# The first projection of a three-layer transformer step on one core: activations split straight out of PSUM, router product in fp32r, halved first weights, an early table load and eighteen warm-up products

## The reference, cut to what matters

```
xn = rms_norm(h, ln_mix[0])                  # 256 x 1024
splits = [q 1024, kc 256, vc 256, ks 256, vs 256, kw 256, vw 256, gl 48]
q, kc, vc, ks, vs, kw, vw, gl = split(xn @ w_in, splits)    # w_in: 1024 x 2608
gates = sigmoid(gl)                          # 48 gate columns
...
# then: compressed, selected and windowed attention, output projection, experts, ...
```

## Time and profile before

| | us |
|---|---|
| three timed runs | 1280.40, 1281.37, 1281.69 |
| median | 1281.37 |
| span of the profiled execution | 1282.1 |
| TensorE busy in it | 1207.8 (94%) |
| VectorE busy | 973.6 (76%) |
| ScalarE busy | 786.0 (61%) |
| first transpose starts | 6.69 |
| kv0 starts | 18.16 |
| q0 starts | 64.62 |

### The profile page before, as it was taken

The page is one execution under the profiler, slowest core; times in us unless marked ns, Lnnn a source line. Parts: engine busy times, 40 slices in busy tenths (PEclk is TensorE's granted clock), DMA queues, the critical chain, the costliest instruction groups (busy, mean ns, idle before and its releaser), DMA issues.

```text
span 1282.1 us, 15617 instructions
## 1 busy us (share of the span) xinstructions
PE 1207.8 (94%) x5843; PEld 982.8 (77%) x5843; DVE 973.6 (76%) x1347; ACT 786.0 (61%) x1166; POOL 25.2 (2%) x38
## 2 busy tenths in 40 slices
PE   6998998999999888989999998999998999999997
PEld 5887786888887677778788776887786887888886
DVE  4977848898987877779989886777777877675545
ACT  6467747677777677667777777443436566544343
POOL 0000000000000000000000000000001001000000
PEclk8998999999999999999999998999999999999999
DMA  8660213798996511339989935777785624467420
GB/s 318 242 264 1 66 67 140 289 370 343 357 372 236 230 71 67 137 142 386 363 346 368 349 116 209 287 284 287 290 327 230 258 120 146 167 278 286 164 99 34
DMA packets 41467, 291.84 MB, mean 228 GB/s; under 512 B 4736, under 2 KB 5120, under 8 KB 6576
## 3 DMA queue, kind: packets, MB, share of 16 engines
q1 hardware_dynamic: 40464, 287.82, 58.5%
q0 software_dynamic: 784, 2.63, 0.7%
q10 hardware_dynamic: 144, 0.39, 0.1%
HBM read 289.78 MB, written 1.05 MB: 227 GB/s over the span
## 4 chain that ended last, share of the span: by engine, by line
PE 62%; DVE 19%; ACT 10%; DMA 4%; issue 4%; POOL 0%; DVEq 0%; ACTq 0%; POOLq 0%
PE ps L430 17%; PE ps L432 17%; PE ps L431 17%; DVE wl L1659 6%; ACT wh L1173 4%; DMA ring<-stream_dram 4%; DVE AR L1889 3%; PE ps L625 1%; ACT AR L1295 1%; ACT XN L1196 1%; PE ps L985 1%; PE ps L458 1%; PE ps L578 1%; PE ps L626 1%; ACT XH L1228 1%
## 5 line engine op out<-in xcount | busy, mean ns | idle before, releaser
L1659 DVE TENSOR_TENSOR wl<-ring,wh 128x2048 fp32r<-128x2048 f32 x229 | 525.6, 2302 | 141.4 <-ACT wh L1173 138.0
L1173 ACT ACTIVATE wh<-ring 128x2048 fp32r<-128x2048 f32 x229 | 437.7, 1915 | 132.2 <-PE ps L432 67.2
L430 PE MATMUL ps<-wh,XH 128*128 128x512 f32 x1040 | 419.1, 403 | 13.0 <-DVE wl L1659 5.2
L432 PE MATMUL ps<-wh,XL 128*128 128x512 f32 x1040 | 408.0, 392 | 0.0
L431 PE MATMUL ps<-wl,XH 128*128 128x512 f32 x1040 | 407.1, 391 | 0.0
L430 PEld LDWEIGHTS ps<-wh,XH 128*128 128x128 f32 x1040 | 196.3, 189 | 61.6 <-issue 8.9
L432 PEld LDWEIGHTS ps<-wh,XL 128*128 128x128 f32 x1040 | 196.2, 189 | 43.0
L431 PEld LDWEIGHTS ps<-wl,XH 128*128 128x128 f32 x1040 | 196.7, 189 | 37.7 <-issue 0.7
L430 PE MATMUL ps<-wh,HT 128*128 128x512 f32 x360 | 142.0, 395 | 8.4 <-DVE XL L2085 4.5
L432 PE MATMUL ps<-wh,HT 128*128 128x512 f32 x360 | 140.4, 390 | 0.0
L431 PE MATMUL ps<-wl,HT 128*128 128x512 f32 x360 | 140.2, 389 | 0.0
(11 more groups left out here) (304 smaller groups left out, 1257.5 us busy)
## 6 DMA issues: line engine op xcount, KB each, us to landing
ring<-stream_dram SPq DMA_DIRECT2D x272, 1024.0 KB, 5.6
H<-x_dram SPq DMA_DIRECT2D x2, 512.0 KB, 4.9
out_dram<-XN SPq DMA_DIRECT2D x4, 256.0 KB, 2.0
XN<-ag_dram POOLq DMA_DIRECT2D x1, 768.0 KB, 5.1
AR<-pT_dram POOLq DMA_DIRECT2D x2, 256.0 KB, 2.9
AR<-g_final_dram POOLq DMA_DIRECT2D x1, 512.0 KB, 4.8
C<-cols_dram ACTq DMA_DIRECT2D x1, 385.0 KB, 4.6
ring<-stream_dram SPq DMA_DIRECT2D x2, 144.0 KB, 5.5
```

Source lines behind the costliest of these rows:

```text
L430: e.matmul(o, ah, bh, start=start, stop=False)
L432: return e.matmul(o, al, bh, start=False, stop=stop)
L1173: e.activation(wh[:, k % WBUF, :], ring[:, n % RING, :], ACT.Copy, scale=1.0).then_inc(up("whi", ("whi", k)))
L1659: e.tensor_tensor(wl[:, k % WBUF, :], ring[:, n % RING, :], h.bitcast(F32), ALU.subtract).then_inc(up("wlo", ("wlo", k)))
```

## The change

The transposes go on as before (`turn_rows`), but with no `XF` for this stage. ScalarE writes `XH = gain * bank` straight in fp32r (`high_all`), VectorE writes `XL = gain * bank - XH` straight from the bank (`low_all`, eight instructions in place of sixteen). The gates' weights are split too (`router_high`, `router_low`, 128x384), and their product is 24 fp32r products of 48 by 256 in place of the float32 one (`narrow_split`). Chunk 1 is split in two halves on ScalarE and VectorE, and kv0 begins behind the first half. The small activation that loads the square-root table stands at the head of ScalarE's program, before the wait for `cols`. TensorE issues 18 products of the identity with itself behind the wait for `cols` and ahead of the wait for x. Turning the gates back moves behind kv0. On ScalarE the copies of kv0 and the sigmoid and SiLU instructions now stand ahead of the third `take`, which splits chunk 5.

```diff
+WARM = 18
+        def router(n, part):
+            return TT_[:, 8 * n * part:8 * n * part + 8 * n]
 # tensor_program
-            def weights():
+            def weights(halved=False):
                 k = split_no[next_chunk()]
-                e.wait_ge(*at("wlo", k))
+                e.wait_ge(*(at("wlo half", k) if halved else at("wlo", k)))
...
+            def turn_rows(name, ready):
+                for label in ready:
+                    e.wait_ge(*at(*label))
+                for j in range(4):
+                    b = bank("fm", name, j, by=[("xs", name, 2 * j + 1)])
+                    for u in range(2):
+                        for t in range(TT):
+                            ins = e.transpose(b[:, 256 * u + 128 * t:256 * u + 128 * t + 128], H[:, t, 2 * j + u:D:8], ID)
+                    ins.then_inc(up("full", ("fm", name, j)))
+            def narrow_split(name, n):
+                next_chunk()
+                h, lo = (router(n, i).rearrange("p (t n) -> p t n", t=8) for i in range(2))
+                b = bank("narrow", name, by=[("nr", name)])
+                e.wait_ge(*at("rwl", name))
+                for k in range(8):
+                    e.wait_ge(*at("xs", name, k))
+                    ins = mm3(b[0:n, 0:256], (h[:, k, :], lo[:, k, :]), (XH[:, k, :], XL[:, k, :]), k == 0, k == 7)
+                ins.then_inc(up("full", ("narrow", name)))
...
 # project
+                            if halved and i + t == 0 and u == 2:
+                                e.wait_ge(*at("wlo", k))
 # tensor nsa()
-                feature_major_all("mix0", [("x", 0), ("x", 1)])
-                narrow("mix0", 48)
-                narrow_rows("mix0", 48, [("gt", 1)])
+                for i in range(WARM):
+                    e.matmul(PS[7][:, 0:128], IDR[:, :], IDR[:, :], start=True, stop=True)
+                turn_rows("mix0", [("x", 0), ("x", 1)])
+                narrow_split("mix0", 48)
...
-                project("kv0", "mix0", lambda t: [("kv", 0, t)])
+                project("kv0", "mix0", lambda t: [("kv", 0, t)], halved=True)
+                narrow_rows("mix0", 48, [("gt", 1)])
 # scalar_program
+            def high_all(name, gain, n, groups):
+                for i in groups:
+                    if i % 2 == 0:
+                        e.wait_ge(*at("fm", name, i // 2))
+                    e.activation(XH[:, i, :], ps("fm", name, i // 2)[:, 256 * (i % 2):256 * (i % 2) + 256], ACT.Copy,
+                                 scale=gain[:, i:i + 1]).then_inc(up("xraw", ("xh", name, i)))
+            def router_high(name, n, c):
+                e.wait_ge(*at("land", c))
+                e.activation(router(n, 0), ring[:, c % RING, 0:8 * n], ACT.Copy, scale=1.0).then_inc(up("act", ("rwh", name)))
+            def narrow_out(name, n):
+                e.wait_ge(*at("narrow", name))
+                e.activation(NR[0:n, :], ps("narrow", name)[0:n, 0:256], ACT.Copy, scale=1.0).then_inc(up("act", ("nr", name)))
 # scalar nsa()
-                feature_major_all("mix0", col("mix0", 0, 8))
-                narrow("mix0", 48)
+                high_all("mix0", col("mix0", 0, 8), 48, range(2))
+                router_high("mix0", 48, 0)
+                high_all("mix0", col("mix0", 0, 8), 48, range(2, 8))
+                n, more = chunks.due(AHEAD)
+                split_half(n, 0, 1)
+                split_half(n, 1, 1)
+                split([more])
+                narrow_out("mix0", 48)
                 split(chunks.one())
-                rms("mix0", lambda t, hf: ("x", t))
+                for t in range(TT):
+                    squares("mix0", t, lambda hf: ("x", t))
+                roots("mix0")
+                take()
+                e.wait_ge(*at("rs", "mix0"))
+                for t in range(TT):
+                    e.wait_ge(*at("pj", "kv0", t))
+                    e.activation(KV[:, t, half(0)], ps("pj", "kv0", t)[:, :], ACT.Copy, scale=rs(t)).then_inc(up("act", ("kv", 0, t)))
                 e.wait_ge(*at("rows", "mix0"))
-                e.wait_ge(*at("rs", "mix0"))
                 gv = ps("rows", "mix0")[:, 0:96].rearrange("p (a n) -> p a n", a=2)
...
-                kv_part(0)
+                take()
                 kv_part(1)
...
             e.wait_ge(*at("ident"))
+            warm("mix0")
             e.wait_ge(*at("cols"))
 # vector_program
+            def low_all(name, gain, groups):
+                for i in groups:
+                    e.wait_ge(*at("xh", name, i | 1))
+                    e.scalar_tensor_tensor(out=XL[:, i, :], in0=ps("fm", name, i // 2)[:, 256 * (i % 2):256 * (i % 2) + 256], scalar=gain[:, i:i + 1],
+                                           in1=XH[:, i, :].bitcast(F32), op0=ALU.mult, op1=ALU.subtract).then_inc(up("xsplit", ("xs", name, i)))
+            def router_low(name, n, c):
+                e.wait_ge(*at("rwh", name))
+                e.tensor_tensor(router(n, 1), ring[:, c % RING, 0:8 * n], router(n, 0).bitcast(F32), ALU.subtract).then_inc(up("dve", ("rwl", name), ("raw", c)))
 # vector nsa()
-                feature_major_all("mix0")
-                take()
+                low_all("mix0", col("mix0", 0, 8), range(2))
+                router_low("mix0", 48, 0)
+                low_all("mix0", col("mix0", 0, 8), range(2, 8))
+                n, more = chunks.due(AHEAD)
+                split_half(n, 0, 1)
+                split_half(n, 1, 1)
+                split([more])
                 split(chunks.one())
                 rms("mix0")
```

More of the change, by code:

```diff
@@ L496, in project_by_tile, with project @@
                             ins.then_inc(up("full", *labels))
-            def project(name, x, by, of=tuple(range(8)), between=None, part=(0, 1)):
+            def project(name, x, by, of=tuple(range(8)), between=None, part=(0, 1), halved=False):
                 if 0 in part:
@@ L503, in project @@
                 for i in part:
-                    k, h, l = weights()
+                    k, h, l = weights(halved and i == 0)
                     hv, lv = (v.rearrange("p (t n) -> p t n", t=4) for v in (h, l))
@@ L1481, in kv_part @@
                         e.activation(KV[:, t, half(c)], b[:, :], ACT.Copy, scale=rs(t)).then_inc(up("act", ("kv", c, t)))
-                        if c:
-                            e.activation(SQ[:, t, 256 * c - 256:256 * c], b[:, 0:256], ACT.Square, scale=rs(t)).then_inc(up("act", ("kvsq", c, t)))
+                        e.activation(SQ[:, t, 256 * c - 256:256 * c], b[:, 0:256], ACT.Square, scale=rs(t)).then_inc(up("act", ("kvsq", c, t)))
                 def first_layer(i):
```

## The result

| | before | changed |
|---|---|---|
| median, us | 1281.90 (10 runs) | 1285.07 (10 runs) |
| range | 1279.08 to 1284.20 | 1284.01 to 1286.32 |
| ratio | | 1.0020, 95% interval 1.0012 to 1.0028 |
| profiled execution: span | 1282.1 | 1283.7 (its own time 1285.76, so 2.06 lie around the span) |

The change is 3.2 us slower (1.5 to 3.6 by the interval) where 1.8 us faster was forecast. The forecast had given 0.08 to anything slower than 1283.9. In the profiled executions of all runs 2.0 to 2.2 us lie around the span, so the one of before, 1282.1, stood for 1284.1 to 1284.3, level with the two slowest of its ten (1284.08 and 1284.20). It was no typical execution.

A forecast was written before the change was run, and what follows sets the result against it. TensorE was taken to bound up to q0, VectorE 2.0 us behind. Start 1.9 + clock 3.1 - gates 0.25 - chunk 5 2.3 - VectorE at q0 0.45 = 1.95, rounded to 1.8: 1279.6 us, range 1277.9 to 1282.6.

The forecast's parts named there:

- the delay of the transposes: On TensorE ahead of kv0: 18 warm-ups end at 9.24, 2.55 us behind the arrival of x, and delay the transposes.
- the ready time of chunk 5: Second half of kv1: its split and low part are ready 8.0 us after the end of kv0.
- the wait of 2.3 us: In the middle of kv1: TensorE stands still 2.3 us for chunk 5, now split behind the copies of kv0.
- VectorE's bound at q0: At q0: VectorE has the first low part ready only at 62.65, TensorE would be there at 62.2; 0.45 us lost.
- Rival A: Ahead of kv0: warm-ups are cheap, 0.107 us each, kv0 starts at 15.45; gain 2.75 us, 1278.6; chance 0.25.
- Rival C: In kv0: the clock isn't held, kv0 begins at half clock, 3.1 us lost; 1282.5 us; chance 0.15.
- 3.1 (clock): In kv0: full clock in place of the half clock at its start gains 3.1 us.
- rival B: Behind the wait in kv1: the clock falls, TensorE loses 1.7 to 3.1 us; 1280.7 to 1282.1; chance 0.3.
- the likeliest case: Whole kernel: the summed terms hold, 1279.6 us (1278.9 to 1280.5); chance 0.3.
- the headline of my sum: At the end of kv0: 27.2 against 32.2, 5.0 us earlier, 1.9 by start and 3.1 by clock.

The follow-up runs named there:

- after_again: The changed kernel run once more with no edit, for a second profiled execution; median 1285.05 us, ratio to before 1.0020.
- before_late: The kernel before, with only ScalarE's copies of kv0, sigmoids and SiLU moved ahead of the split of chunk 5; 1287.15 us, ratio to before 1.0041.
- no_warm: The changed kernel without the 18 warm-up products (WARM = 0); median 1284.24 us, ratio to before 1.0013.
- before_third: The kernel before, no edit, third profiled execution; 1280.10 us (1 run).
- before_again: The kernel before run once more with no edit, for a second profiled execution; median 1282.55 us, ratio 1.0005.

## Why the prediction was wrong

**What held.** The warm-ups at 0.213 us each (0.215), their end at 9.24 (9.47), the delay of the transposes, XL at 0.40 start to start, kv0 at 16.3 (16.51) to 27.2 (27.5), full clock in kv0, the ready time of chunk 5 (8.0 us behind the end of kv0; 35.8 - 27.5 = 8.3), the wait of 2.3 us (2.3), VectorE without idle time from 33.6 to 58, VectorE's bound at q0 (0.45 us in the sum, 0.3 in after_again). The transposes ended near 12.8 and not at 11.8, since the clock rose later than at 10.7, and this cost nothing. Rival A fell: the warm-ups are not cheap. Taking them away gave what A had worked out for the start of kv0 (15.45; 15.40), by way of `kr`. Rival C didn't occur in any of the three executions, nor in the five of the variants with the changed start.

**The step that failed first: "3.1 (clock)".** The mechanism was right and the size was not. I took the 6.14 us of half clock in the one profile of before as a property of the kernel. In four executions the half clock was 6.8, 3.4, 0 and 3.4 us long, worth some 3.1, 1.7, 0 and 1.7 in kv0, a mean of 1.6 (1.3 with before_late, whose kv0 ran at full clock). With 1.6 the sum gives some 0.5 us in place of 1.95 (its printed terms add up to 2.00): no change. A warning was on record: the span alone already lay 0.7 us above the median of the timed runs, and I took off only 0.15 for it; with the 2.0 to 2.2 us that lie around a span it was 2.8.

**The second: rival B against the likeliest case.** I gave 0.3 to each and put the price of B outside the sum. The clock fell behind the wait in two of three executions (two of four with no_warm) and cost 1.7 us (7.16 against 5.5 us for 24 products); at q0 that is 1.4 us later, since VectorE covers the rest.

**The sum done over at q0.** The forecast moved q0 from 64.62 to 62.65, 1.97 us earlier. The mean of before is 62.79, which takes away 1.83: 1.6 by clock and start of kv0, and 0.24 because 64.62 was the end of the instructions before q0, while q0's first product starts at 64.38. Without a fall of the clock the changed kernel has q0 at 63.18, 0.53 later than forecast: some 0.3 is the later end of kv0, and 0.25 passes between the end of the low part (60.64 + 2.29 = 62.93) and the product, for which the sum had nothing. The fall adds 1.37 in two of three, 0.91 on average. Together -1.97 + 1.83 + 0.53 + 0.91 = +1.30, the measured difference.

**What makes the change slow** is therefore one part of it, the order on ScalarE. Shown by two edits: with chunk 5 split early the change gives 4.1 us (early_take), and the late split put alone into before costs 5.2 (before_late). The sum had priced this wait rightly, at 2.3 us and its follow-up at q0; what it lacked was a gain large enough to pay for it. With the early split the rest is worth 0.18% (0.10 to 0.27%), of which the start is little: early_take reaches q0 0.6 us ahead of before_third, the execution of before at full clock; the other 1.7 us against the mean of before are that kv0 met no low clock in any of the eight executions with the changed start. So the headline of my sum, 5.0 us at the end of kv0, was 4.5 against one execution and is 3.0 against the mean of four (kv1's first product at 32.06, 30.37, 28.79 and 30.70).

**What stays open.** From q0 to 218 us the traces of before and of the changed kernel run in parallel within 0.1 us. At q0 the changed kernel is 1.3 us behind (standard error 0.8), in total 2.5 (1.4 to 3.7; after_again) to 3.2 us. The difference of 1.2 to 1.9 us lies later. In the profiled executions the changed kernel takes 0.9 us longer from q0 to the end of the span (1218.5 against 1217.6 on average, standard error 0.4). Behind q0 the executions of before have three or four falls of the clock and those of the changed kernel five each, not all in the same places. Two windows of TensorE alone, changed kernel first, the first profile of before second (busy, instructions, clock, DMA share, GB/s):

```profile
219.00:229.00 10.00, 7.61 (x29) 0.83 0.09 19
...
779.00:792.00 13.00, 8.68 (x40) 1.00 0.77 285
```

```profile
219.00:229.00 10.00, 7.76 (x37) 1.00 0.10 25
...
779.00:792.00 13.00, 9.23 (x34) 0.74 0.47 174
```

Which idle stretches are followed by a fall differs between executions of one kernel here too. The first profile of before is the odd one again, for the other three of before do fall in the first window; before_again:

```profile
219.00:229.00 10.00, 7.75 (x30) 0.83 0.27 95
```

The mean granted clock of the timed runs is the same, 0.991 for both kernels, which speaks against more half clock as the cause. Whether the rest is real or the error of means from four and three executions was not settled.

## What to carry to other kernels

When an eviction is pulled ahead of other work on an in-order engine, list what it jumps over and when each of those is due: here one 1.9 us copy moved behind two copies, two sigmoids and two table loads, and took back everything that the other edits had won. Warm-up products for TensorE that run on beyond the arrival of the first real operand delay the first real instruction in full, here by 2.8 us, and can still bring full clock no sooner. And a clock stretch read from one profile is a draw: take a second profile of the kernel before, or hold the profiled execution's time against the timed runs, before a term rests on it.

## What the hardware showed that I had not expected

- The same program, the same instructions: the fall of the granted clock ahead of kv0 came in three of four executions, for 3.4 or 6.8 us. In the 4 us that end at kv0 TensorE was busy for 0.32, 1.06, 1.72 and 0.85 us, and for 1.86 in before_late; the two busiest went without a fall (there the gates' product had run at half clock for longer, 4.7 us in place of 3.8 to 3.9). Behind the wait of 2.3 us it fell in two of four, no_warm counted.
- The granted clock reads 1.00 until its first change, but the first transposes and the warm-ups run at half pace: 0.215 us for a product of 128 columns with its load, against 0.11 later.
- Transposes alone were followed by full clock: in no_warm the clock records have it from 10.0 us on, when TensorE had run nothing but its 16 transposes from 6.74 (3.53 us for the sixteen, against 3.65 in before).
- A fp32r product of 48 rows by 256 columns takes 0.117 us at full clock (24 starts from 13.03 to 15.71), no less than one with 128 rows of output (18 in 2.29 us, with the tail of the last).
